# Projections of a hybrid layer: two shared 252-column halves in one 504-column matmul, with an add on VectorE

## What is computed

```python
def hybrid_layer(x, c, ...):
    mod = silu(c) @ w_ada + b_ada                       # shifts, scales, gates
    h = modulate(rms_norm(x, g_pre_mix), shift_m, scale_m)
    u, q, k, v, z_pool, z_att = split(h @ w_in)         # 1024 -> 7680
    y_pool = pool_mix(u_ext, pos, w_pool_map, pool_scale) @ w_proj_pool
    o = merge_groups(three dilated window attentions)   # 8 slots of 64
    y_att = o @ w_proj_att
    mix = (sigmoid(z_pool) * y_pool + sigmoid(z_att) * y_att) @ w_out
    x = x + gate_m * rms_norm(mix, g_post_mix)
    h = modulate(rms_norm(x, g_pre_ffn), shift_f, scale_f)
    hc = b_conv + sum_j hu_ext[:, j:j + T] * w_conv[j]  # hu = h @ w_up, 1024 -> 5632
    a, b = split(hc)
    x = x + gate_f * rms_norm((gelu(a) * b) @ w_down, g_post_ffn)
```

## Time and profile before

| | |
|---|---|
| runs, us | 1154.72, 1158.25, 1155.15; median 1155.15 |
| profiled execution, us | 1152.73, its span 1150.9 |
| mean granted TensorE clock | 0.953 |
| TensorE matmuls busy | 1060.8 us, 92% |
| VectorE, ScalarE, GpSimd busy | 480.6, 422.1, 129.3 us |
| instructions on TensorE | 8663 matmuls, each with a weight load |

### The profile page before, as it was taken

The page is one execution under the profiler, slowest core; times in us unless marked ns, Lnnn a source line. Parts: engine busy times, 40 slices in busy tenths (PEclk is TensorE's granted clock), DMA queues, the critical chain, the costliest instruction groups (busy, mean ns, idle before and its releaser), DMA issues.

```text
span 1150.9 us, 20622 instructions
## 1 busy us (share of the span) xinstructions
PE 1060.8 (92%) x8663; PEld 991.8 (86%) x8663; DVE 480.6 (42%) x873; ACT 422.1 (37%) x675; POOL 129.3 (11%) x173
## 2 busy tenths in 40 slices
PE   5589999999999999979989697399999999999996
PEld 3489999999999999967857696399999999999994
DVE  1533423332433243353742433755656565622224
ACT  4334322442244224434301232454444444422222
POOL 4000210030004000503601300300000000000000
PEclk9599999999999999989989898599999999999997
DMA  9777577757775777225752336246666666455312
GB/s 324 258 263 254 194 234 239 234 171 231 239 238 163 236 243 233 87 89 169 238 172 68 107 93 232 75 157 219 222 224 223 222 224 224 143 174 166 112 39 74
DMA packets 226809, 216.02 MB, mean 188 GB/s; under 512 B 6125, under 2 KB 191853, under 8 KB 226701
## 3 DMA queue, kind: packets, MB, share of 16 engines
q1 hardware_dynamic: 226717, 214.70, 57.2%
HBM read 207.27 MB, written 96.03 MB: 264 GB/s over the span
## 4 chain that ended last, share of the span: by engine, by line
PE 86%; DVE 5%; POOL 3%; ACT 3%; issue 2%; DMA 1%; SPq 0%; POOLq 0%; ACTq 0%; DVEq 0%
PE acc L1258 73%; PE psT L1531 2%; PE psS L1294 2%; POOL ssq L576 2%; PE psS L1403 2%; PE psT L1417 2%; POOL tha L618 1%; PE psS L1302 1%; PE psS L1391 1%; PE psT L1431 1%; PE acc L1323 1%; PE psS L1389 1%; PE psS L1507 1%; DVE xT L1202 1%; DMA vec_rows<-in_b_conv 1%
## 5 line engine op out<-in xcount | busy, mean ns | idle before, releaser
L1258 PE MATMUL acc<-act_hi,w_hi 128*128 128x260 f32 x1824 | 377.7, 288 | 20.2 <-DVE act_lo L1107 7.2
L1258 PE MATMUL acc<-act_hi,w_lo 128*128 128x260 f32 x1824 | 369.8, 284 | 0.0
L1258 PE MATMUL acc<-act_lo,w_hi 128*128 128x260 f32 x1824 | 369.6, 284 | 0.0
L879 DVE TENSOR_TENSOR w_lo<-raw,w_hi 128x1024 fp32r<-128x1024 f32 x150 | 191.7, 1279 | 374.3 <-ACT w_hi L637 373.7
L1258 PEld LDWEIGHTS acc<-act_hi,w_hi 128*128 128x128 f32 x1824 | 283.9, 191 | 27.5 <-issue 22.6
L1258 PEld LDWEIGHTS acc<-act_lo,w_hi 128*128 128x128 f32 x1824 | 284.0, 190 | 0.0
L1258 PEld LDWEIGHTS acc<-act_hi,w_lo 128*128 128x128 f32 x1824 | 283.8, 190 | 0.0
L637 ACT ACTIVATE w_hi<-raw 128x1024 fp32r<-128x1024 f32 x150 | 156.9, 1047 | 202.6 <-PE acc L1258 196.4
L1258 PE MATMUL acc<-g_hi,w_hi 128*128 128x260 f32 x352 | 71.0, 283 | 0.0
L1258 PE MATMUL acc<-g_hi,w_lo 128*128 128x260 f32 x352 | 70.8, 282 | 0.0
L1258 PE MATMUL acc<-g_lo,w_hi 128*128 128x260 f32 x352 | 70.6, 282 | 0.0
(11 more groups left out here) (243 smaller groups left out, 1143.9 us busy)
## 6 DMA issues: line engine op xcount, KB each, us to landing
out_k_sample<-in_cache_k_w SPq DMA_DIRECT2D x89, 368.0 KB
out_v_sample<-in_cache_v_w SPq DMA_DIRECT2D x89, 368.0 KB
raw<-in_w_in SPq DMA_DIRECT2D x60, 512.0 KB, 6.0
raw<-in_w_up SPq DMA_DIRECT2D x44, 512.0 KB, 5.6
ada_mid<-in_w_ada SPq DMA_DIRECT2D x11, 1024.0 KB, 10.2
ada_first<-in_w_ada SPq DMA_DIRECT2D x9, 1024.0 KB, 10.7
raw<-in_w_down SPq DMA_DIRECT2D x16, 512.0 KB, 3.9
out_k_sample<-in_cache_k_w SPq DMA_DIRECT2D x16, 511.0 KB
```

The costliest lines, as they stand in the source:

```text
L879: dve.tensor_tensor(w_lo[:, n % HL, 0:cols], raw[:, n % RAW, 0:cols], w_hi[:, n % HL, 0:cols].bitcast(F32), ALU.subtract).then_inc(lo_read ...
L1258: ins_ = pe.matmul(acc[b][:, half, 0:HALF], w, x[:, t, half * HALF:(half + 1) * HALF], start=first and i == 0 and j == 0, stop=last and i ...
```

## The change

The matmuls of a weight tile become five. The first 268 tokens (LEFT) are handled as before, with three matmuls of 268 columns into the first bank. For the other 252 tokens the high weight multiplies the high and the low activations in one matmul of 504 columns, whose two results lie side by side in the accumulator at columns 520 to 1023 (`acc_parts`); the low weight's matmul of 252 columns adds to the first of the two. High and low activations are laid out as one tensor for this. Before anything reads a sum, VectorE adds the two sums of 252 columns into columns 268 to 519 (`add_low`, one TENSOR_REDUCE over two values each, out of PSUM and into PSUM) and signals `whole`; the 520 columns of a sum then lie together. ScalarE waits for `whole` where it waited for TensorE, and VectorE, where it reads sums, waits for its own add.

```diff
-HALF = TC // 2
+LEFT = 268
...
-        act_hi, act_lo = put("act_hi", [KT, TC], F32R, r_act), put("act_lo", [KT, TC], F32R, r_act + FULL)
+        act2 = put("act", [2, KT, TC], F32R, r_act)
+        act_hi, act_lo = act2[:, 0], act2[:, 1]
...
-        accv = [a[:, :, 0:HALF] for a in acc]
+        acc_flat = [a[:, :, :].rearrange("p a b -> p (a b)") for a in acc]
+        accv = [a[:, 0:TC] for a in acc_flat]
+        acc_parts = [a[:, TC:].rearrange("p (a n) -> p a n", a=2) for a in acc_flat]
...
+        def added(eng, s):
+            eng.wait_ge(whole, SUM[s] + 1)
...
                     if what == "unit":
-                        done(act, s)
+                        added(act, s)
...
+            def add_low(s):
+                b = SUM[s] % 2
+                dve.tensor_reduce(accv[b][:, LEFT:], acc_parts[b].rearrange("p h n -> p n h"), AX_X, ALU.add).then_inc(whole, 1)
...
                     if what == "unit":
+                        done(dve, s)
+                        add_low(s)
                         if k < 9 and k % 3 == 2:
-                            done(dve, s)
+                            added(dve, s)
...
                     for q in range(4):
                         i = 4 * m + q
+                        if q < 3:
+                            dve.wait_ge(part_done, 3 * m + q + 1)
+                        else:
+                            done(dve, u)
+                        add_low(("map", i))
                         dve.wait_ge(mixed_hid, i + 1)
...
+                        add_low(("pa", i))
+                        added(dve, ("pa", i))
...
                 for half in range(2):
                     s, e = ("up", i, half), 2 * i + half
+                    done(dve, s)
+                    add_low(s)
                     evacuated(dve, s)
...
                 for part in range(3):
                     split(N["down", m, part] + 2)
+                done(dve, ("down", m, 2))
+                add_low(("down", m))
                 add_square(("down", m), 24, m)
...
-            def blocks(s, slot, pairs, hi, lo, first=True, last=True):
+            def blocks(s, slot, pairs, both, first=True, last=True):
                 b = SUM[s] % 2
+                left, pair = acc[b][:, 0, 0:LEFT], acc_parts[b]
+                right = pair[:, 0, :]
                 for i, (blk_, t) in enumerate(pairs):
                     wh, wl = w_hi[:, slot, blk_ * P:(blk_ + 1) * P], w_lo[:, slot, blk_ * P:(blk_ + 1) * P]
-                    for j, (w, x) in enumerate(((wh, hi), (wh, lo), (wl, hi))):
-                        for half in range(2):
-                            ins_ = pe.matmul(acc[b][:, half, 0:HALF], w, x[:, t, half * HALF:(half + 1) * HALF],
-                                             start=first and i == 0 and j == 0, stop=last and i == len(pairs) - 1 and j == 2)
+                    start, stop = first and i == 0, last and i == len(pairs) - 1
+                    if not stop:
+                        pe.matmul(pair, wh, both[:, :, t, LEFT:TC], start=start, stop=False)
+                    pe.matmul(left, wh, both[:, 0, t, 0:LEFT], start=start, stop=False)
+                    pe.matmul(left, wh, both[:, 1, t, 0:LEFT], start=False, stop=False)
+                    pe.matmul(right, wl, both[:, 0, t, LEFT:TC], start=False, stop=False)
+                    ins_ = pe.matmul(left, wl, both[:, 0, t, 0:LEFT], start=False, stop=stop)
+                    if stop:
+                        ins_ = pe.matmul(pair, wh, both[:, :, t, LEFT:TC], start=False, stop=True)
                 return ins_
```

More of the change, by code:

```diff
@@ L769, in _ @@
                         i = 4 * m + q
[L770 to L774, removed]
+                        added(act, ("map", i))
+                        act.activation(mix_hi[:, i, :], of(("map", i)), ACT.Identity, scale=vec[:, 80 + i:81 + i]).then_inc(mixed_hid, 1)
                 if (what, m) == ("pp", 6):
@@ L1183, in _ @@
             for m in range(8):
+                done(dve, ("out", m, 0))
+                add_low(("out", m))
                 split(N["out", m, 0] + 2)
@@ L1360, in _ @@
                     for k in range(2):
-                        ins_ = blocks(("pair", 0, k), first[k], [(t, t)], act_hi, act_lo, first=t == 0, last=t == KT - 1)
+                        ins_ = blocks(("pair", 0, k), first[k], [(t, t)], act2, first=t == 0, last=t == KT - 1)
                         if t == KT - 1:
@@ L1461, in _ @@
                             take(s)
-                            blocks(s, slot, [(i, i) for i in range(KT)], act_hi, act_lo).then_inc(unit_done, 1)
+                            blocks(s, slot, [(i, i) for i in range(KT)], act2).then_inc(unit_done, 1)
                     elif what == "v":
@@ L1553, in _ @@
                         take(("map", i))
-                        ins_ = blocks(("map", i), slot, [(4 * (q // 2) + 2 * kt + d, 2 * g + kt) for kt in range(2)], act_hi, act_lo)
+                        ins_ = blocks(("map", i), slot, [(4 * (q // 2) + 2 * kt + d, 2 * g + kt) for kt in range(2)], act2)
                         ins_.then_inc(unit_done if q == 3 else part_done, 1)
@@ L1565, in _ @@
                         evacuated(pe, ("map", 7))
-                    blocks(("pp", m), slot, [(i, i) for i in range(KT // 2)], mix_hi, mix_lo, last=False)
+                    blocks(("pp", m), slot, [(i, i) for i in range(KT // 2)], mix2, last=False)
                     if pos < 7:
@@ L1572, in _ @@
                         sample_values()
-                    blocks(("pp", m), slot, [(i, i) for i in range(KT // 2, KT)], mix_hi, mix_lo, first=False).then_inc(unit_done, 1)
+                    blocks(("pp", m), slot, [(i, i) for i in range(KT // 2, KT)], mix2, first=False).then_inc(unit_done, 1)
                     if m == 6:
@@ L1582, in _ @@
                         take(("pa", 2 * m + q))
[L1583 removed]
+                        ins_ = blocks(("pa", 2 * m + q), slot, [(2 * kt + q, kt) for kt in range(4)], o2)
                         ins_.then_inc(unit_done if q else part_done, 1)
@@ L1597, in _ @@
                     pe.wait_ge(merged_split, 8)
-                blocks(("out", m), slot, [(i, i) for i in range(KT)], act_hi, act_lo).then_inc(unit_done, 1)
+                blocks(("out", m), slot, [(i, i) for i in range(KT)], act2).then_inc(unit_done, 1)
                 if m >= 4:
@@ L1620, in _ @@
                             pe.wait_ge(act_split, 8 + k + 1)
-                            ins_ = blocks(s, slot, [(k, k)], act_hi, act_lo, first=k == 0, last=k == KT - 1)
+                            ins_ = blocks(s, slot, [(k, k)], act2, first=k == 0, last=k == KT - 1)
                     else:
-                        ins_ = blocks(s, slot, [(k, k) for k in range(KT)], act_hi, act_lo)
+                        ins_ = blocks(s, slot, [(k, k) for k in range(KT)], act2)
                     ins_.then_inc(unit_done, 1)
@@ L1634, in _ @@
                     t0 = 8 * part
-                    blocks(("down", m), slot, [(i, t0 + i) for i in range(min(8, FT - t0))], g_hi, g_lo, first=part == 0, last=part == 2).then_inc(unit_done, 1)
+                    blocks(("down", m), slot, [(i, t0 + i) for i in range(min(8, FT - t0))], g2, first=part == 0, last=part == 2).then_inc(unit_done, 1)
                 if m == 5:
```

51 lines of the change are left out of this document (27 added, 24 removed).

## The result

The changed kernel takes 1168.35 us (median of four runs, 1166.66 to 1169.45), the kernel before 1154.93 (1153.63 to 1158.25): ratio 1.0121, 95% interval 1.0086 to 1.0156. It is slower by 1.2%, where 0.6% faster was forecast. The profiled execution took 1169.45 us, its span is 1167.6, 16.7 us more than the span before. The medians differ by 13.4: the profiled execution of the kernel before, 1152.73 us, is 2.2 under the median of its kernel, that of the changed one 1.1 over.

A forecast was written before the change was run, and what follows sets the result against it. TensorE's projection stream was taken as bound by weight loads, one per matmul. Tiles -18.2, w_up -2.4 and added path +14.2 gave -6.4 us, from 1152.73 to 1146.3, plus 2.4 for the median: 1148.5 us; eight-in-ten range 1140 to 1172.

The forecast's parts named there:

- the other four stay bound by loads at 120.2 ns: Projection weight tile: its four shorter matmuls keep 120.2 ns each, the weight load's length, as 268 columns are only 112.
- The 18.2 us of 768 tiles: Pair, down, out and pp stages: each weight tile goes from 721 to 698 ns, saving 23.7 ns.
- 337 - 117: Row of 512-column matmuls: 337 ns between starts less 117 taken as the first's own load, giving 220 ns.
- some 12 ns to hand its weights over: Projection matmuls: added to a load's stream of some 107 ns, it makes a load as long as a 120 ns matmul.
- Rival 1: Projection matmuls: each has a fixed cost, not a load's bound; a tile saves 12 ns, 1157.5 us; chance 0.17.
- Rival 2: VectorE's add: jumping reads cost double, 1.07 us an add, so VectorE bounds w_up; 1172 us; chance 0.2.
- Rival 3: Adds hide better at 0.6 us and loads bound fully, so tiles save 28 ns; 1140.5 us; chance 0.08.
- Rival 4: PE's idle times at map and start lower the clock more, or a pair seam opens; 1153 to 1158; chance 0.1.
- forecast -2.4: w_up stage: VectorE's loop of 11.43 us sets the pace instead of PE's 11.54, so 22 pairs save 0.11 us each.
- 0.5 as a chance: Start: should PE's idle 4.4 us bring the clock to 1.2 GHz, some 16 to 30 matmuls cost about 100 ns more.
- The three ends: Ends of the pair, out and down stages: the add lengthens the path by 0.7 us each, 2.1 in all.
- 3.4 forecast: Map stage: VectorE's add, wait and low part take 2.2 us a sum; four groups lose 0.7, 1.0, 0 and 1.7.

The follow-up runs named there:

- The probes: Two runs of the kernel before with rows of matmuls, one kind to a row, added behind its last work; 1273.89 us and 1306.03 us, one run each.

## Why the prediction was wrong

**The failed step** is "the other four stay bound by loads at 120.2 ns", with "220 ns for 512 columns". A matmul in fp32r takes 0.45 to 0.46 ns for each column at 2.4 GHz, from 252 to 512 columns, instead of the 0.417 that the clock gives, and a row bound by loads has 111 ns for one, less than the 116.7 of the shortest matmul here. The kernel before was bound by columns all along, and the change leaves their number at 1560. The stream after is 714 to 718 ns a tile (forecast 698): 230 ns for 504 columns instead of 217, and four others of 124, 124, 124 and 116 instead of 120.2. The 18.2 us of 768 tiles are 2.3, by the table of tiles (464 x 2.0 + 64 x 3.8 + 64 x 2.6 + 176 x 5.7 ns). The probes show the rate with nothing else running, so it isn't contention between engines.

**How the rows misled.** 337 - 117 took two records of the earlier trace rows and a guess about the inside of the first. In an unbroken row the same 56-row matmul of 512 columns takes 233 ns, 13 more. The other support, 106 ns between two loads plus "some 12 ns to hand its weights over", named a number that no row had. One reading of the earlier trace rows was open and not weighed: 24 matmuls at 1.2 GHz took 219 ns, 1% over the columns, while at 2.4 GHz it is 11% over; a cost in proportion to the columns that comes only at 2.4 GHz fits that as well as a load does. It is also what the probes show.

**The rivals.** Rival 1, a fixed cost of 11.9 ns per matmul, is false too: 504 columns pay 23 ns over 210, 260 pay 12 over 108; what a matmul fewer saved is 2 to 6 ns. By it the result would have been 1157.5. The figure of the Trainium skill ("TensorE: Matmul & The Clock Gate", section on the back-to-back issue gap), N/2.4 + 2.5 ns, gives 212.5 for 504 columns: the bf16 row has 212.5 and agrees, the fp32r row has 233 and does not. For the change its consequence, 2.5 ns saved per tile, was near what the tiles show, where I had 23.7. Rival 2 forecast 1172, next to the result, and its mechanism is false: the add that jumps takes 0.689 us, not 1.07. Rival 3 fell with the loads. Rival 4 was real in part: TensorE's clock falls at the start, which costs 1.4 us. It falls in the map too, but there it also does in executions of the kernel before. Two sums of the prediction are slightly off: rival 3 comes to 1148.5 - 3.3 - 4.9 = 1140.3, and the length of an add from which the change loses to 0.68 + 6.4/61 = 0.785 us instead of 0.77.

**The add.** 0.68 forecast, 0.689 measured over 144. The exception of the Trainium skill ("Vector Engine (DVE) Microarchitecture Reference", section 5.2) for one stream alternating between two regions is what the row shows; the slow copy of the earlier trace rows was no guide to it.

**w_up**, forecast -2.4, measured +2.9. VectorE's loop was taken as 11.43 us and is 11.45 where it waits for no sum (from the add at 824.06 us to that at 835.51); the step that failed is again PE's pace, 11.44 and not 11.16. With two loops of nearly one length the adds make some w_lo late, PE restarts at a cost of up to some 0.4 us, and the pair takes 11.56 and 11.78 us in turn. With the add moved the stage has 256.33 us, as without any add, 2.0 less than before: near the 2.4 of the forecast, but by PE's pace and not by VectorE's.

**On the path elsewhere.** pa: 5.7 forecast, 5.9 measured. The start: 2.3 and 2.3; the chain after shows the forecast steps:

```profile
70.11 0.69 DVE hist_sum L980 x3
70.81 0.61 DVE acc L895
...
71.94 1.06 ACT w_hi L645
...
73.02 1.24 DVE w_lo L885
...
74.30 0.49 PE acc L1287
```

The clock's part, "0.5 as a chance": 1.4 us. After 4.3 us without a matmul (69.16 + 0.84 to 74.30) TensorE's clock goes to 1.2 GHz at 75.3 for 3.4 us, and a 268-column matmul then takes 220 ns, as in this timeline of PE:

```profile
75.63 0.43 PE L1289 MATMUL acc<-act,w_hi 128*128 128x268 f32 x1
75.85 0.41 PE L1290 MATMUL acc<-act,w_lo 128*128 128x252 f32 x1
```

The three ends: 0.7 each forecast; 0.95 measured at the pair stage, 0.74 from the last matmul of "out" to the next stage, 0.73 from the last of "down" to the end. That "out" as a whole is shorter than before comes from its matmuls, 1.4 us less with the shorter time at 1.2 GHz. pp: 0.2 forecast, 1.0 measured, which one execution can't tell from nothing. map: 3.4 forecast, 4.8 measured, of which by the kernel without adds only 1.6 are the adds. Against the execution of the kernel before with two falls (27.04) it is 1.9. The rest goes with the clock, which falls to 1.2 GHz twice for 3.4 us here too (522.4 and 536.1). In the timeline the first fall follows an idle time of 4.59 us:

```profile
522.55 0.76 PE L1287 MATMUL acc<-act,w_hi 128*128 128x504 f32 x1 [4.59 <-DVE mixed L1132]
523.11 0.43 PE L1288 MATMUL acc<-act,w_hi 128*128 128x268 f32 x1
```

PE pauses in the map even where no add stands in the way, before too (2.42 us for a low part). So the sum as it should have been: tiles -2.3, w_up +2.9, elsewhere 5.9 + 1.9 + 2.3 + 1.4 + 2.4 = +13.9 (pa, map, the start and its clock, the three ends) where 14.2 were forecast, and by the clock the norm's -0.9 and out's -1.2: near +12.4, for the 13.4 between the medians. The 16.7 of the spans have some 3 us more by the two falls in the map, which the profiled execution before did not have. The costs elsewhere were right but for the map, forecast 1.5 to 1.8 too high, and the clock at the start, 0.9 too low; the gain of 18.2 was 2.3.

## What to carry to other kernels

Joining two matmuls into one saves the difference between what each streams and what bounds it; before counting on it, take the start-to-start time of two lengths from the trace (or from a short row of them) and see whether it goes with the columns. An addition that every eviction waits for costs its length wherever its engine stands on the round from sum to weights, and little where the engine waits anyway: here the same 144 adds cost 17 us in one order and 3 to 4 in another. Two loops of nearly one length (11.44 and 11.45 us) do not run at the longer one: the pair took 11.68. And before a difference of 3 us in one stage is put down to a change, look at a second execution of the old kernel: here it held as much.

## What the hardware showed that was not expected

- fp32r at 2.4 GHz streams a column in 0.45 to 0.463 ns (0.417 by the clock) with 128, 64 and 56 rows and on an idle chip; at 1.2 GHz there is no such surcharge (427 ns for 512 columns in the probes, 426.7 by the clock; 219 for 260, 216.7 by the clock); bf16 has 2.5 ns a matmul (212.5 ns for 504 columns, 210 by the clock). Zeros take 227 to 231. What causes it stays open.
- A row of 128- or 192-column matmuls in fp32r takes 111 ns each, which I read as the load's bound.
- After a pause of 4.3 us at the start the clock was down for 3.4 us. With the adds moved it was too, after a pause of only 2.09 us behind the transposes of the history; after 2.01 us in the kernel before (three executions) and in the one without adds it was not. What decides between the two isn't known.
- In the map the same kernel had no, one and two falls of the clock in three executions, and the stage took 24.18, 25.72 and 27.04 us.
